# Selection of attended keys spread over the attention, and a feed-forward whose down projections lag one inner unit behind

## The chip, the cores and the metric

One core of a Trainium2 chip runs the whole program once. The metric is the time on the device in microseconds (us). PE is TensorE, DVE is VectorE, ACT is ScalarE, POOL is GpSimd, SP is SyncE.

## The reference

Two layers of a decoder trunk are applied to 1024 prompt tokens and 32 sample tokens (8 sequences of 4). Cut to what the change touches:

```
sc   = indexer_scores(q_idx, w_idx, k_idx)          # relu scores, weighted heads
sc   = where(key_pos <= pos, sc, -inf)
_, idx = top_k(sc, 256)                              # keys each token may attend
o    = softmax(q k[idx]^T / 8) v[idx]                # 8 query heads, 2 KV heads
...
x    = x + g1 * (concat[A, B, C] @ w_out)
h2   = rmsnorm(x) * (1 + sc2) + sh2
x    = x + g2 * (silu(h2 @ w_gate) * (h2 @ w_up)) @ w_down      # D = 1024, 2816 inner
```

`top_k` takes the earlier key where scores are equal. The kernel gathers no prompt keys: it adds a mask of 0 or -1e30 to dense logits.

## The kernel before, in words

All activations stand transposed: 8 tiles of 128 features by 1056 tokens, in three column chunks of 352 (TC). Each engine has its own instruction stream, and the order is written out by hand with semaphores. One loop runs over the two layers. `ended(engine, l, k)` (line 614) is a fence between stages: ACT and DVE each mark it, and whoever waits goes on only when both have. PSUM banks 0 to 2 form ring A, which ACT reads, and banks 3 to 5 ring Dr, which DVE reads; PE's `open` waits for a free bank, in order.

**Search.** For each token the 256th largest score is found bit by bit in 34 passes, on DVE (L1878) and ACT (L1403), for six blocks of prompt tokens (widths 384 to 1024; the first two blocks attend everything) and one array of sample scores (width 1056). It gives a threshold `thr` and `need`, how many keys equal to the threshold are still admitted.

**Selection.** Then DVE walks SEL_ORDER (L1945 to L1961), the sample first and after it the blocks from narrow to wide. For each it marks the scores equal to the threshold (L1952, for the sample L1949, with a count that PE sums over segments), numbers them with a scan (L1953), keeps those within `need` (L1957) and adds those above the threshold (L1960). ACT turns each result into a mask, (selected - 1) * 1e30, written over the scores (L1415). All three engines then pass fence 7 before the attention begins.

**Attention.** 32 turns p, block b = 7 - p//4, so from the widest block to the narrowest, four turns a block, one for each pair of heads. PE: `qk(p+1)` (L1071), `turns(p)` (transposes of the probabilities, L667), `pv(p-1)` (L1097), and from turn MASK_AT = 23 on `mask` (L1119), which expands the sample's mask. DVE: `logits(p+1)` (L1976: bank plus mask to SBUF, with the maximum), `turned(p)` (L1987), now and then `scales` and `heads`. ACT: `turned(p)` (L1432), `probs(p+1)` (exponentials, L1423). POOL meanwhile issues gathers of cached value rows, in order; the first four wait for the last use of the sample's key logits buffers.

**Products.** `product` (L703) multiplies 8 or nf tiles of 128 x 128 weights by 352 columns, three matmuls each (hi*hi, hi*lo, lo*hi of split fp32), chunk by chunk. The raw weights come by SP into one of two places; ACT writes their hi part (L1235) and DVE their lo part (L1512), and `unit_used`, counted by PE, says that the place's hi and lo parts are free again. `pair_by_tile` (L738) runs the first two products after a norm side by side, tile by tile, as the tiles of h arrive: once for w_in and once for the first gate and up products, in each layer.

**Feed-forward.** 22 inner units (gate product into ring A, up product into ring Dr), in blocks (0, 8), (8, 8), (16, 6) of FF_BLOCKS. For a unit ACT takes Silu of each gate chunk (L1473), DVE multiplies by the up chunk (L2089), ACT writes g_hi (L1478) and DVE g_lo (L2094), each into one of 8 tile slots. After a block PE waits for `g_ready`, which DVE marks behind the last g_lo, and then runs 8 down products over the block's tiles into ring Dr, which DVE adds to x (L2057).

Of the kernel before, what the change touches and what calls it, by code (L numbers as in the profile page):

```python
# [9 lines left out]
ALU = mybir.AluOpType  # L10
# [4 lines left out]
P = 128  # L15
# [14 lines left out]
BIG = 1e30  # L30
# [18 lines left out]
SEL_ORDER = (6, 0, 1, 2, 3, 4, 5)  # L49
# [119 lines left out]
FF_BLOCKS = ((0, 8), (8, 8), (16, 6))  # L169
TILES = 3 * KD + 3 * KF  # L170
UNITS = 18 + KD + sum(2 * n + KD for _, n in FF_BLOCKS)
# [122 lines left out]
def build(nc, a, o):  # L294
    ctx = ExitStack()
    with ctx:
# [87 lines left out]
        O_ROWIN, O_RMS, O_ACC, O_SQ = R(14), R(15), R(24), (R(22), R(21))  # L384
# [10 lines left out]
        MASK_USED = (1, 3, 4, 6)  # L395
        MASK_AT = 32 - 9
# [30 lines left out]
        def _(sp):  # L427
# [28 lines left out]
            with loop(sp, DEPTH, [units]) as l:  # L456
# [22 lines left out]
                for f0, nf in FF_BLOCKS:  # L479
                    with loop(sp, nf, [units]) as i:  # L480
                        unit(0, (to(0, KD, P), layer(wg, l)[:, :, bass.ds(i * P + f0 * P, P)]))
                        unit(1, (to(1, KD, P), layer(wu, l)[:, :, bass.ds(i * P + f0 * P, P)]))
# [6 lines left out]
        def _(pool):  # L489
# [30 lines left out]
            with loop(pool, DEPTH, [outs]) as l:  # L520
# [136 lines left out]
        def _(pe):  # L657
# [35 lines left out]
            def product(n, ring, hi, lo, n_k=KD):  # L693
# [3 lines left out]
                for c in range(3):  # L697
                    bank = ring.open()
                    for k in range(n_k):
                        w = slice(n % 2 * UNIT + k * P, n % 2 * UNIT + k * P + P)  # L700
                        x = slice(k * TOK + c * TC, k * TOK + c * TC + TC)
# [24 lines left out]
            def pair_by_tile(hi, lo, tiles):  # L726
# [4 lines left out]
                for k in range(KD):  # L731
                    pe.wait_ge(tile_lo, tiles + k + 1)
                    for u, ring in enumerate((A, Dr)):
                        w = slice(u * UNIT + k * P, u * UNIT + k * P + P)
                        for c in range(3):
                            x = slice(k * TOK + c * TC, k * TOK + c * TC + TC)
                            for m, (wt, xt) in enumerate(((w_hi, hi), (w_hi, lo), (w_lo, hi))):
                                mm = pe.matmul(banks[u][c][:, 0:TC], wt[:, w], xt[:, x], start=(k + m == 0), stop=(k == KD - 1 and m == 2))  # L738
                                if k == KD - 1 and u == 1 and c + m == 0:
                                    mm.then_inc(unit_used, 1)  # L740
                            if k == KD - 1:
                                ring.close(mm)
# [51 lines left out]
            with loop(pe, DEPTH, counts) as l:  # L794
# [268 lines left out]
                ended(pe, l, 7)  # L1063
# [58 lines left out]
                for p in range(32):  # L1122
# [7 lines left out]
                    if p >= MASK_AT:  # L1130
                        mask(p - MASK_AT)
# [60 lines left out]
                for f, (f0, nf) in enumerate(FF_BLOCKS):  # L1192
# [953 lines left out]
```

## Time and profile before

| | |
|---|---|
| three timed runs | 3782.92 to 3783.92 us, median 3783.87 |
| the profiled execution | 3765.66 us, its span 3763.8 |
| granted TensorE clock, mean | 0.91 of full speed |
| chain that ended last | PE 73%, DVE 9%, issue 7%, ACT 4%, DMA 4% |
| on that chain, L703 (products) | 53% |
| first layer: search, selection, attention | 590 to 752, 752 to 786, 786 to 947 us |
| first layer: feed-forward from the pair on | 1109 to 1885 us |

Read it so: the shares say that PE's products are most of the chain, but PE is busy 85% of the span, and the rest is spread over stages. What a change in a stage is worth is read from that stage's own stretch. The profiled execution ran 18 us under the median of the timed ones.

### The profile page before, as it was taken

How to read it: one execution, taken by the hardware profiler on the slowest of the kernel's cores; microseconds unless marked ns; L12 is line 12 of the kernel's file. 1: busy time of each engine (PE TensorE's matmuls, PEld its weight loads, DVE VectorE, ACT ScalarE, POOL GpSimd, SP SyncE). 2: the span in 40 equal slices, each digit the busy share in tenths (PEclk: the TensorE clock that was granted, in tenths of full speed). 3: DMA queues.
4: the chain of work that ended last, by engine and by line, in shares of the span. 5: the costliest groups of instructions: out<-in, count | busy, mean ns of one | idle time of the engine just before them, and what ended most of it. 6: DMA issues, size and time to landing. Idle time of an engine off the chain costs nothing.

```text
span 3763.8 us, 58485 instructions
## 1 busy us (share of the span) xinstructions
PE 3199.0 (85%) x20553; PEld 2738.8 (73%) x20553; DVE 1604.3 (43%) x3497; ACT 1182.9 (31%) x2081; POOL 258.6 (7%) x319
## 2 busy tenths in 40 slices
PE   3997677759889999999989867774889899999995
PEld 3994443235789999999979634332659899999995
DVE  3325568965342222222343355797534322222233
ACT  3122237835323212112231222584542321121121
POOL 1001022100200000000000101310020000000000
PEclk8997679979899999999999866897979899999997
DMA  5115025400411111111122321451041111111111
GB/s 178 39 39 198 12 77 171 145 7 18 169 34 45 45 45 50 40 50 43 42 48 43 112 109 47 140 163 45 18 158 45 34 45 45 45 48 47 45 38 53
DMA packets 275990, 261.19 MB, mean 69 GB/s; under 512 B 85513, under 2 KB 237567, under 8 KB 274513
## 3 DMA queue, kind: packets, MB, share of 16 engines
q1 hardware_dynamic: 244496, 155.76, 13.8%
q0 software_dynamic: 31312, 103.20, 8.4%
q8 instruction: 90, 1.47, 0.2%
q14 instruction: 92, 0.75, 0.1%
HBM read 249.33 MB, written 9.78 MB: 69 GB/s over the span
## 4 chain that ended last, share of the span: by engine, by line
PE 73%; DVE 9%; issue 7%; ACT 4%; DMA 4%; POOL 1%; DVEq 0%; ACTq 0%; SPq 0%; POOLq 0%
PE bank L703 53%; PE bank L667 4%; PE bank L738 2%; PE bank L1071 2%; ACT arena L1403 2%; PE bank L1097 2%; DMA weights<-in_w_ada 2%; DVE arena L1878 2%; PE bank L883 1%; DMA arena<-in_x_sample 1%; PE bank L1119 1%; PE bank L749 1%; PE bank L811 1%; PE bank L719 1%; PE bank L949 1%
## 5 line engine op out<-in xcount | busy, mean ns | idle before, releaser
L703 PE MATMUL bank<-h_hi,w_hi 128*128 128x352 f32 x2784 | 904.5, 325 | 9.8 <-DVE w_lo L1512 9.8
L703 PE MATMUL bank<-h_lo,w_hi 128*128 128x352 f32 x2784 | 894.4, 321 | 0.0
L703 PE MATMUL bank<-h_hi,w_lo 128*128 128x352 f32 x2784 | 894.2, 321 | 0.0
L703 PEld LDWEIGHTS bank<-h_hi,w_hi 128*128 128x128 f32 x2784 | 523.8, 188 | 12.6 <-issue 7.9
L703 PEld LDWEIGHTS bank<-h_lo,w_hi 128*128 128x128 f32 x2784 | 524.8, 188 | 1.7
L703 PEld LDWEIGHTS bank<-h_hi,w_lo 128*128 128x128 f32 x2784 | 523.3, 188 | 0.0
L1512 DVE TENSOR_TENSOR w_lo<-weights,w_hi 128x1024 fp32r<-128x1024 f32 x188 | 230.2, 1225 | 625.5 <-ACT w_hi L1235 620.0
L703 PE MATMUL bank<-g_hi,w_hi 128*128 128x352 f32 x1392 | 452.3, 325 | 16.6 <-DVE arena L610 16.6
L703 PE MATMUL bank<-g_lo,w_hi 128*128 128x352 f32 x1392 | 448.9, 322 | 0.0
L703 PE MATMUL bank<-g_hi,w_lo 128*128 128x352 f32 x1392 | 448.4, 322 | 0.0
L1235 ACT ACTIVATE w_hi<-weights 128x1024 fp32r<-128x1024 f32 x188 | 198.8, 1057 | 635.4 <-PE bank L703 583.0
L667 PEld LDWEIGHTS bank<-arena 128*128 128x128 f32 (+4 forms) x1773 | 216.3, 154 | 227.5 <-issue 174.5
L667 PE MATMUL bank<-arena 128*128 128x128 f32 (+4 forms) x1773 | 281.0, 299 | 112.7 <-DMA arena<-in_x_sample 23.8
L2057 DVE SCALAR_TENSOR_TENSOR stream<-bank,arena,stream 128x352 f32<-128x352 f32 (+1 forms) x192 | 109.6, 572 | 424.9 <-PE bank L703 417.1
L703 PEld LDWEIGHTS bank<-g_hi,w_hi 128*128 128x128 f32 x1392 | 263.1, 189 | 18.3 <-issue 18.3
L703 PEld LDWEIGHTS bank<-g_lo,w_hi 128*128 128x128 f32 x1392 | 263.7, 189 | 0.0
L703 PEld LDWEIGHTS bank<-g_hi,w_lo 128*128 128x128 f32 x1392 | 263.1, 189 | 0.0
L1878 DVE TENSOR_SCALAR_CACHE_REDUCE arena<-arena,srch 128x1056 bf16<-128x1056 int16 (+7 forms) x272 | 226.4, 884 | 11.8 <-DVE srch L1907 10.4
L1403 ACT ACTIVATE arena<-arena,srch 128x1024 bf16<-128x1024 int16 (+5 forms) x204 | 209.7, 1032 | 30.0 <-DVEq L1924 12.5
L2089 DVE TENSOR_TENSOR arena<-arena,bank 128x352 f32<-128x352 f32 x132 | 68.9, 522 | 314.1 <-PE bank L703 312.9
L1478 ACT ACTIVATE g_hi<-arena 128x352 f32 x132 | 65.8, 498 | 402.3 <-DVEq L2090 402.3
L1071 PE MATMUL bank<-arena 64*128 64x512 f32 (+3 forms) x384 | 95.7, 577 | 95.5 <-ACT arena L612 63.5
(327 smaller groups left out, 3711.4 us busy)
## 6 DMA issues: line engine op xcount, KB each, us to landing
weights<-in_w_ada SPq DMA_DIRECT2D x64, 512.0 KB, 7.0
weights<-in_w_gate SPq DMA_DIRECT2D x44, 512.0 KB, 3.7
weights<-in_w_up SPq DMA_DIRECT2D x44, 512.0 KB, 3.7
weights<-in_w_in SPq DMA_DIRECT2D x72, 256.0 KB, 3.5
arena<-in_w_ada SPq DMA_DIRECT2D x32, 512.0 KB, 4.3
weights<-in_w_down SPq DMA_DIRECT2D x32, 512.0 KB, 3.7
arena<-in_w_ada SPq DMA_DIRECT2D x8, 1024.0 KB, 18.2
weights<-in_w_down SPq DMA_DIRECT2D x16, 384.0 KB, 3.4
```

Source lines behind the costliest of these rows:

```text
L667: return pe.transpose(out, in_, C("ident", n, 0, 0, n))
L703: mm = pe.matmul(bank[:, 0:TC], wt[:, w], xt[:, x], start=(k + m == 0), stop=(k == n_k - 1 and m == 2))
L738: mm = pe.matmul(banks[u][c][:, 0:TC], wt[:, w], xt[:, x], start=(k + m == 0), stop=(k == KD - 1 and m == 2))
L1071: Dr.close(pe.matmul(banks[g][:, 0:w], S(R(R_Q + i, b * P), P, 64 * g, 64), S(R(R_K, c0), w, 64 * g, 64), start=True, stop=True))
L1097: mm = pe.matmul(B((XB, YB)[done % 2], [[1, P]], P * i, 64 * g, 64), S(O_VT + P * k + 64 * g, 64), S(O_PTT[p % 2][g] + P * k, P), start=(k ...
L1235: act.activation(w_hi[:, w], S(O_W + n % 2 * UNIT, UNIT), ACT.Copy).then_inc(unit_hi, 1)
L1403: act.activation(junk, digits(j, i), ACT.Sign, bias=srch[:, 0, j:j + 1], scale=-1.0, accum_out=S(M_CNT + j, 1)).then_inc(sign_counted, 1)
L1478: act.activation(g_hi[:, bass.ds(i * TOK + c * TC, TC)], S(R(17, c * TC), TC), ACT.Copy).then_inc(tile_hi, 1)
L1512: dve.tensor_tensor(w_lo[:, w], S(O_W + n % 2 * UNIT, UNIT), w_hi[:, w].bitcast(F32), ALU.subtract).then_inc(unit_lo, 1)
L1878: ins = dve.tensor_scalar(junk, digits(j, i), cand[:, j:j + 1], None, ALU.is_lt, ALU.add, accum_out=S(M_RAW if j == 6 else M_CNT + j, 1))
L2057: ins = dve.scalar_tensor_tensor(out=x, in0=bank[:, 0:w], scalar=S(O_MOD + 9 * (gate + j), 1), in1=x, op0=ALU.mult, op1=ALU.add)
L2089: read(dve.tensor_tensor(S(R(17, c * TC), TC), S(R(16, c * TC), TC), bank[:, 0:TC], ALU.mult))
```

## The change

The selection of the widest block alone stands before the attention; the others run in steps between DVE's attention turns (SEL_STEP), and ACT negates each in turn 2, 6, 10, 14, 18 or 22. PE no longer waits at fence 7. The scratch moves to four slots of the arena (R(5) to R(8)), where cached value rows were gathered early, so the first four value gathers now wait for the last mask. The feed-forward's blocks become (tiles of the down products) 7, 7, 8, with 8, 7, 7 inner units ahead of them, the tiles wrapping around the 8 slots. `pair_by_tile` runs the last two tiles of the first product before those of the second, and frees the first place when the second product's last two begin. The rows of the next layer's parameters land in R(23) instead of R(14).

```diff
-SEL_ORDER = (6, 0, 1, 2, 3, 4, 5)
+SEL_ORDER = (5, 4, 3, 2, 1, 0, 6)
+SEL_STEP = {0: ((1, 0), (1, 1)), 1: ((1, 2), (1, 3))}
+for _m in range(2, 7):
+    for _k in range(4):
+        SEL_STEP[4 * _m - 6 + _k] = ((_m, _k),)
-FF_BLOCKS = ((0, 8), (8, 8), (16, 6))
+FF_BLOCKS = ((0, 7, 8), (7, 7, 7), (14, 8, 7))
-        O_ROWIN, O_RMS, O_ACC, O_SQ = R(14), R(15), R(24), (R(22), R(21))
+        O_ROWIN, O_RMS, O_ACC, O_SQ = R(23), R(15), R(24), (R(22), R(21))
+        O_EQ, O_CUM, O_GT, O_EQS = (R(5 + n) for n in range(4))
...
                     if n < 4:
-                        pool.wait_ge(s_kv_used, l * 64 + 8 + K_TILES)
+                        pool.wait_ge(neg_ready, l * 7 + 7)
...
-                for k in range(KD):
-                    pe.wait_ge(tile_lo, tiles + k + 1)
-                    for u, ring in enumerate((A, Dr)):
...
-                                if k == KD - 1 and u == 1 and c + m == 0:
+                turns = [(k, u) for k in range(KD - 2) for u in range(2)] + [(k, u) for u in range(2) for k in range(KD - 2, KD)]
+                for k, u in turns:
+                    ring = (A, Dr)[u]
+                    if u == 0:
+                        pe.wait_ge(tile_lo, tiles + k + 1)
...
+                            if k == KD - 2 and u == 1 and c + m == 0:
+                                mm.then_inc(unit_used, 1)
...
                 count(PASSES, "earlier_seg", M_RAW + 1)
-                ended(pe, l, 7)
...
                     if p >= MASK_AT:
+                        if p == MASK_AT:
+                            pe.wait_ge(neg_ready, l * 7 + 7)
                         mask(p - MASK_AT)
...
-                for f, (f0, nf) in enumerate(FF_BLOCKS):
+                for f, (f0, nf, nu) in enumerate(FF_BLOCKS):
                     settle(pe)
-                    with loop(pe, nf - (f == 0), counts) as i:
+                    with loop(pe, nu - (f == 0), counts) as i:
                         product(0, A, h_hi, h_lo)
                         product(1, Dr, h_hi, h_lo)
                     pe.wait_ge(g_ready, l * 3 + f + 1)
                     settle(pe)
                     with loop(pe, KD // 2, counts) as i:
                         for n in range(2):
-                            product(n, Dr, g_hi, g_lo, nf)
+                            product(n, Dr, g_hi, g_lo, nf, f0 % KD)
...
-                for m, j in enumerate(SEL_ORDER):
+                def negated(m):
+                    j = SEL_ORDER[m]
                     act.wait_ge(sel_ready, l * 7 + m + 1)
-                    act.activation(neg_s if j == 6 else score(j), S(R(20 + m % 2), TOK if j == 6 else P * (j + 3)), ACT.Copy, bias=-BIG, scale=BIG).then_inc(neg_ready, 1)
+                    act.activation(neg_s if j == 6 else score(j), S(O_CUM, TOK if j == 6 else P * (j + 3)), ACT.Copy, bias=-BIG, scale=BIG).then_inc(neg_ready, 1)
+                negated(0)
                 ended(act, l, 7)
...
                 for p in range(32):
+                    if p % 4 == 2 and p < 24:
+                        negated(p // 4 + 1)
                     turned(p)
...
+                def select(m, k):
+                    j = SEL_ORDER[m]
+                    sc, n = score(j), P * (j + 3)
+                    eq, cum = S(O_EQ, n), S(O_CUM, n)
+                    if k == 0:
...
+                        step(dve.tensor_scalar(eq, sc, thr[:, j:j + 1], None, ALU.is_equal))
+                    elif k == 1:
+                        if m:
+                            dve.wait_ge(neg_ready, l * 7 + m)
+                        step(dve.tensor_tensor_scan(cum, eq, eq, 0.0, ALU.add, ALU.max))
+                    elif k == 2:
+                        step(dve.scalar_tensor_tensor(out=eq, in0=cum, scalar=need[:, j:j + 1], in1=eq, op0=ALU.is_le, op1=ALU.mult))
+                    else:
+                        dve.scalar_tensor_tensor(out=cum, in0=sc, scalar=thr[:, j:j + 1], in1=eq, op0=ALU.is_gt, op1=ALU.add).then_inc(sel_ready, 1)
+                def select_sample(k):
+                    eq, cum = S(O_EQS, TOK), S(O_CUM, TOK)
+                    if k == 0:
+                        dve.wait_ge(neg_ready, l * 7 + 6)
+                        step(dve.tensor_tensor_scan(cum, eq, eq, 0.0, ALU.add, ALU.max))
+                    elif k == 1:
+                        step(dve.scalar_tensor_tensor(out=eq, in0=cum, scalar=need[:, 6:7], in1=eq, op0=ALU.is_le, op1=ALU.mult))
+                    elif k == 2:
+                        dve.tensor_tensor(cum, eq, S(O_GT, TOK), ALU.add).then_inc(sel_ready, 1)
+                step(dve.tensor_scalar(S(O_EQS, TOK), score(6), thr[:, 6:7], None, ALU.is_equal, ALU.add, accum_out=S(M_RAW + 1, 1)))
+                dve.sem_inc(count_raw, 1)
+                for k in range(4):
+                    select(0, k)
+                step(dve.tensor_scalar(S(O_GT, TOK), score(6), thr[:, 6:7], None, ALU.is_gt))
+                dve.wait_ge(count_sum, (l + 1) * (PASSES + 1))
+                step(dve.tensor_tensor(need[:, 6:7], need[:, 6:7], XB[:, 0:1], ALU.subtract))
                 ended(dve, l, 7)
...
                 def logits(p):
                     b, i, done = PAIRS[p]
                     full = P * (b + 1)
+                    if i == 0 and b > 1:
+                        dve.wait_ge(neg_ready, l * 7 + NB - b)
...
                         heads(p // 4 - 1)
+                    for m, k in SEL_STEP.get(p, ()):
+                        if m < 6:
+                            select(m, k)
+                        else:
+                            select_sample(k)
...
+                def hidden(u, i, slot, signal=False):
...
+                    if signal:
+                        mark(dve, g_ready)
+                    split_lo(1)
+                for f, (f0, nf, nu) in enumerate(FF_BLOCKS):
+                    first = f0 + f
+                    if f == 2:
+                        hidden(f0 + 1, 0, KD - 1)
+                    whole = nf - 1 - min(f, 1) - (f == 2)
+                    with loop(dve, whole, counts) as i:
+                        hidden(first, i, i)
+                    hidden(first + whole, 0, whole, True)
+                    if f < 2:
+                        hidden(first + whole + 1, 0, whole + 1)
```

`hidden` on ACT and on DVE is the body of a unit as it was, with the tile's slot given by hand. SP's loops fetch the weights in the new order: 8, 7 and 7 gate and up pairs, and down products of 7, 7 and 8 tiles.

## Rows read from the trace of the kernel before

**Rows 1.** The page: busy time of the engines, share of the 3763.8 us span.

```profile
PE 3199.0 (85%) x20553; PEld 2738.8 (73%) x20553; DVE 1604.3 (43%) x3497; ACT 1182.9 (31%) x2081; POOL 258.6 (7%) x319
```

**Rows 2.** Stretches: us; busy PE, PEld, DVE, ACT, POOL; clock, DMA share, GB/s.

```profile
752.30:786.00 33.70, 0.58 (x2) 0.50 (x2) 31.29 (x33) 5.92 (x8) 0.00 (x0) 0.50 0.02 6
786.00:947.00 161.00, 139.46 (x1200) 88.26 (x1201) 84.49 (x320) 90.29 (x220) 4.50 (x5) 0.93 0.05 14
2574.00:2607.00 33.00, 0.58 (x2) 0.50 (x2) 30.90 (x31) 5.70 (x7) 0.00 (x0) 0.50 0.01 3
```

**Rows 3.** In order of time: start, us, engine, line, tiles, idle before and its releaser.

```profile
752.30 1.30 DVE L1949 TENSOR_SCALAR_CACHE_REDUCE arena<-arena,code 128x1056 f32<-128x1056 f32 x1
753.76 2.36 DVE L1953 TENSOR_TENSOR_SCAN arena<-arena 128x1056 f32<-128x1056 f32 x1
...
773.78 0.69 DVE L1952 TENSOR_SCALAR arena<-arena,code 128x896 f32<-128x896 f32 x1
...
776.56 1.15 DVE L1957 SCALAR_TENSOR_TENSOR arena<-arena,srch 128x896 f32<-128x896 f32 x1
...
778.93 0.75 DVE L1952 TENSOR_SCALAR arena<-arena,code 128x1024 f32<-128x1024 f32 x1
...
784.69 1.06 ACT L1415 ACTIVATE arena<-arena 128x1024 f32<-128x1024 f32 x1 [4.80 <-DVE arena L1960]
...
785.93 0.17 DVE L1964 MEMSET arena<- 128x128 f32 x1 [1.15 <-ACT arena L612]
...
788.34 0.69 DVE L1976 CUSTOM_DVE_ANT_0 arena<-bank,arena 128x512 f32<-128x512 f32 x1 [1.99 <-PE bank L1071]
```

**Rows 4.** Waits of DVE and ACT in the attention: total, times, longest.

```profile
DVE arena L1976 <- PE bank L1071: 51.0, 37, 2.4
ACT arena L1432 <- PE bank L667: 57.3, 34, 4.0
```

**Rows 5.** DVE in the attention, in brackets its idle time before the row.

```profile
802.17 0.69 DVE L1976 CUSTOM_DVE_ANT_0 arena<-bank,arena 128x512 f32<-128x512 f32 x1 [0.62 <-PE bank L1071]
...
809.09 0.69 DVE L1976 CUSTOM_DVE_ANT_0 arena<-bank,arena 128x512 f32<-128x512 f32 x1 [2.33 <-PE bank L1071]
...
899.72 0.69 DVE L1976 CUSTOM_DVE_ANT_0 arena<-bank,arena 128x512 f32<-128x512 f32 x1 [0.85 <-PE bank L1071]
...
902.61 0.56 DVE L1976 CUSTOM_DVE_ANT_0 arena<-bank,arena 128x384 f32<-128x384 f32 x1 [1.03 <-PE bank L1071]
...
905.91 0.56 DVE L1976 CUSTOM_DVE_ANT_0 arena<-bank,arena 128x384 f32<-128x384 f32 x1 [1.70 <-PE bank L1071]
...
908.58 0.56 DVE L1976 CUSTOM_DVE_ANT_0 arena<-bank,arena 128x384 f32<-128x384 f32 x1 [0.97 <-PE bank L1071]
```

**Rows 6.** ACT in the attention, before a pair's transposed tiles are copied.

```profile
912.39 0.87 ACT L1432 ACTIVATE arena<-bank 128x384 f32<-128x384 f32 x2 [0.40 <-PE bank L667]
```

**Rows 7.** Value gathers on the POOL queue.

```profile
748.39 0.93 POOL L573 DMA_INDIRECT arena<-in_cache_v,page_idx  x1 [0.30 <-issue]
```

**Rows 8.** Lines on TensorE: the down projections' products.

```profile
L703 PE MATMUL bank<-g_hi,w_hi 128*128 128x352 f32 x1392 | 452.3, 325 | 16.6 <-DVE arena L610 16.6
```

**Rows 9.** Ten us after three of the switches, and after the pair.

```profile
1302.70:1312.70 10.00, 9.92 (x52) 9.93 (x53) 2.25 (x3) 1.06 (x1) 0.00 (x0) 0.83 0.19 54
...
3126.20:3136.20 10.00, 9.96 (x45) 9.96 (x46) 1.81 (x2) 1.06 (x1) 0.00 (x0) 0.69 0.20 54
3406.70:3416.70 10.00, 9.94 (x61) 9.94 (x62) 2.40 (x3) 1.06 (x1) 0.00 (x0) 1.00 0.20 54
1136.80:1146.80 10.00, 9.93 (x46) 9.93 (x47) 3.95 (x7) 4.18 (x6) 0.00 (x0) 0.72 0.36 105
```

**Rows 10.** First layer, the end of the pair (L738) before the feed-forward's inner units.

```profile
1131.01 1.28 ACT L1473 ACT_TABLE_LOAD   x1 [8.03 <-PE bank L738]
...
1136.87 0.66 PE L703 MATMUL bank<-h_hi,w_hi 128*128 128x352 f32 x1 [3.68 <-DVE w_lo L1512]
```

**Rows 11.** The same at the pair before w_in's products.

```profile
109.70 0.42 PE L703 MATMUL bank<-h_hi,w_hi 128*128 128x352 f32 x1 [1.21 <-DVE w_lo L1512]
```

More of the change, by code:

```diff
@@ L168 @@
 K_TILES = NB * OCT
-FF_BLOCKS = ((0, 8), (8, 8), (16, 6))
+FF_BLOCKS = ((0, 7, 8), (7, 7, 7), (14, 8, 7))
 TILES = 3 * KD + 3 * KF
-UNITS = 18 + KD + sum(2 * n + KD for _, n in FF_BLOCKS)
+UNITS = 18 + KD + sum(2 * n + KD for _, _, n in FF_BLOCKS)
 INDEX_CHUNKS = [(b, c, min(512, P * (b + 1) - c)) for b in range(2, 8) for c in range(0, P * (b + 1), 512)]
@@ L478, in _ @@
                          (to(n, 4, P, 4 * P), w[512:1024].rearrange("(i p) n -> p i n", p=P)))
[L479 to L482, printed above, removed]
+                for f, (f0, nf, nu) in enumerate(FF_BLOCKS):
+                    u0 = f0 + (f > 0)
+                    with loop(sp, nu, [units]) as i:
+                        unit(0, (to(0, KD, P), layer(wg, l)[:, :, bass.ds(i * P + u0 * P, P)]))
+                        unit(1, (to(1, KD, P), layer(wu, l)[:, :, bass.ds(i * P + u0 * P, P)]))
                     with loop(sp, KD // 2, [units]) as i:
@@ L691, in _, with product @@
             counts.append(units)
-            def product(n, ring, hi, lo, n_k=KD):
+            def product(n, ring, hi, lo, n_k=KD, first=0):
                 pe.wait_ge(unit_lo, units.at(3))
@@ L2081, in _ @@
                 Dr.restart()
-                for f, (f0, nf) in enumerate(FF_BLOCKS):
-                    for turns in (nf - 1, 1):
-                        with (loop(dve, turns, counts) if turns > 1 else nullcontext(nf - 1)) as i:
-                            split_lo(0)
-                            for c in range(3):
-                                bank = Dr.next()
-                                dve.wait_ge(gate_ready, l * 3 * KF + i * 3 + (3 * f0 + c + 1))
-                                read(dve.tensor_tensor(S(R(17, c * TC), TC), S(R(16, c * TC), TC), bank[:, 0:TC], ALU.mult))
-                                dve.sem_inc(prod_ready, 1)
-                            for c in range(3):
-                                dve.wait_ge(tile_hi, l * TILES + i * 3 + (3 * KD + 3 * f0 + c + 1))
-                                t = bass.ds(i * TOK + c * TC, TC)
-                                step.only(dve.tensor_tensor(g_lo[:, t], S(R(17, c * TC), TC), g_hi[:, t].bitcast(F32), ALU.subtract))
-                            if turns == 1:
-                                mark(dve, g_ready)
-                            split_lo(1)
+                def hidden(u, i, slot, signal=False):
+                    split_lo(0)
+                    for c in range(3):
+                        bank = Dr.next()
+                        dve.wait_ge(gate_ready, l * 3 * KF + i * 3 + (3 * u + c + 1))
+                        read(dve.tensor_tensor(S(R(17, c * TC), TC), S(R(16, c * TC), TC), bank[:, 0:TC], ALU.mult))
+                        dve.sem_inc(prod_ready, 1)
+                    for c in range(3):
+                        dve.wait_ge(tile_hi, l * TILES + i * 3 + (3 * KD + 3 * u + c + 1))
+                        t = bass.ds(slot * TOK + c * TC, TC)
+                        step.only(dve.tensor_tensor(g_lo[:, t], S(R(17, c * TC), TC), g_hi[:, t].bitcast(F32), ALU.subtract))
+                    if signal:
+                        mark(dve, g_ready)
+                    split_lo(1)
```

65 lines of the change are left out of this document (28 added, 37 removed).

## The prediction

> **What bounds the kernel now.** I read the page first: PE is busy 3199 of 3763.8 us [rows 1], so about 565 us of the span are PE's idle time and only a stage's own stretch can tell which of it goes. The table by stretches comes next. Between the search and the attention there is a hole: 33.7 us with PE busy 0.58, while DVE is busy 31.3 [rows 2]; the second layer has the same hole. The order of instructions shows who holds it: DVE alone, from the sample's comparison at 752.30 to the widest block's last step, then ACT's negation at 784.69, the fence at 785.93, and the first logits leave their bank at 788.34, 36.0 us after the start [rows 3]. In the attention behind it PE is busy 139 of 161 us and DVE 84 [rows 2]; DVE stands 51.0 us waiting for PE's logits, in 37 waits of at most 2.4 [rows 4]. That idle time is the cover into which the selection is put. In the feed-forward PE runs without a hole except where it turns from inner units to down products: six waits on DVE's mark, 16.6 us in all, 2.77 each [rows 8], and after the pair, 3.68 us [rows 10].
>
> **The selection, what leaves the path.** Of the 31.3 us in the hole [rows 2] there remain in front: the sample's comparison with its readout, 1.46 (753.76 less 752.30), and the widest block, 5.76 (784.69 less 778.93) [rows 3]. New is the sample's "greater" comparison, costed as its "equal" one, 1.30, plus about 0.2 for the correction of `need`, 0.3 for marks and fence and 0.4 for preparing the small mask. Sum 9.4. ACT's negation of the widest block (1.06) lies beside the "greater" one. PE no longer stands at the fence, so its first logits, which took 2.3 us from 786.06 on, wait in the bank already. The first eviction comes 9.4 instead of 36.0 us after the start: 26.6 us saved in each layer.
>
> **What comes back in the attention.** The moved DVE work is 31.3 less 1.4, 5.7 and 0.2, so 24.0 us, in 23 instructions; with some 0.05 between dependent ones, 25 us. A step costs only what exceeds DVE's idle time before the next logits [rows 5]. Turn 0 gets the 896 wide block's first half, 2.78 (776.56 less 773.78) [rows 3], where 0.62 is idle: 2.2 lost. Turn 1 gets the second half, 2.37, against 2.33: 0.1. Turns 2 to 17 get one step each, the longest a scan of about 1.76 in turn 3, where the waits are like the 2.33 at 809.09; the tightest is turn 17, 0.62 in 0.85: nothing. Turns 18 to 20 get the sample's scan 2.36 and two more steps of about 1.3, with gaps 5.0, where 1.03, 1.70 and 0.97 are idle: 1.3. ACT's six negations take 0.5 to 1.06, where ACT waits 57.3 us in 34 waits before such copies, 1.7 each [rows 4]; but before turn 22's copies only 0.40 is idle [rows 6], so 0.7 for that one and nothing for the others. Together 4.3 us. The bounds: nothing, if PE had slack that I do not see, and 25, if no cover held. I take 4.3, as the idle times were read just where the steps land. Net 22.3 in each layer, 44.6 in both. What a late step holds up: DVE's next logits, behind them ACT's exponentials and PE's transposes. What is late next in front of the attention is DVE still, with its 9.4.
>
> The four value gathers on POOL (0.93 each, the last of them at 748 [rows 7]) now wait for the last mask, about turn 22, and the later ones queue behind them. Four times 1.24 is 5 us of POOL, with 33 us of attention left (912 to 947 [rows 2, 6]) and the DMA at a 0.05 share of its time [rows 2]. Costed at nothing; without that cover they would add 5 to the value stage.
>
> **The feed-forward.** The waits after the first and second block go, since PE has a whole unit (gate and up product, 23 us) to run while DVE finishes the tiles: 2 x 2 x 2.77 = 11.1 us. The third stays, as no unit is left to run ahead. With the waits goes what the clock takes after them: in the ten us after three of the four the granted clock is 0.83, 0.69 and, once, 1.00, with 52, 45 and 61 matmuls [rows 9] (the fourth, at 1582, is like the first). By the missing matmuls, 10 + 10 + 17 at 0.16 each, near 6.2 us more. So the clock was at its lower level, 1.2 GHz, for a time after an idle wait of 2.8, in three cases of these four. The work is otherwise the same: 22 units and 176 tiles of down product. The down products now follow an up product in the same ring, but DVE has read each bank two chunks (over 7 us) before it is wanted again, so nothing is added. More unrolled code on ACT and DVE: I put it at nothing, under the slack of a 11.5 us product.
>
> **The pair.** Ring A closes nine matmuls earlier and the first place is freed nine earlier: 9 x 0.16 = 1.43. In the feed-forward the wait of 3.68 hangs on ACT's table load and Silus, which start when the first gate chunk closes [rows 10], so it falls by 1.43. At w_in the wait of 1.21 [rows 11] hangs on the freed place and goes. Both layers: 2 x (1.43 + 1.21) = 5.3. The lower clock after the pair (0.72 [rows 9]) I leave; if the shorter wait spares it, 1.7 to 2.8 a layer more.
>
> **The sum.** 44.6 + 11.1 + 6.2 + 5.3 = 67.2 us, from the profiled 3765.66 to 3698.5. That execution lies 18.2 under the median of the timed runs; taken from the median, 3783.87 less 67.2 gives 3716.7.
>
> **Rivals.** **A, the selection is only half covered.** The idle times before the logits are not free room: a late eviction also holds back PE's transposes, and the delays add up over the turns. For it: the attention is a ring of three engines in which PE is busy 139 of 161 us, so PE catches up little. Against it: DVE's waits are on PE nearly all [rows 4]. With all 25 us exposed the saving falls by 2 x 20.7 to 25.8, 3758; half of it gives 3737.
> **B, the down projection finds another wait.** The change would not do what it says if the first down product waited for its split weights or for a bank of ring Dr that DVE reads late, since DVE now has a unit's work and the first residual close together. Then 11.1 + 6.2 = 17.3 stay: 3734. Against it: the same weights arrive in time between the products inside a block.
> **C, slower: the clock.** The attention's mean clock is 0.93, so about 22 of its 161 us run at 1.2 and the rest at 2.4 GHz [rows 2]. If the longer holes of turns 0 and 18 kept it at the lower, a wide turn (6.9 us, 802.17 to 809.09 [rows 5]) would take about 5 more, as its logits, transposes and products all double. To eat 33.6 us a layer this must hold for 7 wide turns; held through all the attention, PE's 139 us would grow by over 100 a layer, and the kernel would take about 3920. The trace speaks against it, as the clock stays up through the waits of every turn. The Trainium skill, "TensorE: Matmul & The Clock Gate", under "A second HAM failure mode: psum-queue depth-cycling", tells of a kernel that cycles through PSUM banks with short PE idles in between and so swings between the two clocks; by that rule this change, which adds such idles, risks C. The attention before has these idles already and mostly does not swing.
>
> **Chances.** The forecast 0.71, A 0.13 (in whole or half), B 0.08, C 0.04, the rest for mishaps that cost a few us. The range: down to 3702, if the selection costs nothing (8.6 less) and the clock after the pair is spared (about 5); up to 3738, which takes in B and half of A. A measurement of this kernel can tell about 0.2% from no change, 7.6 us; A and B lie beyond it too, on the faster side: faster 0.94, same 0.02 (A in whole with further losses), slower 0.04 (C).
>
> **What would show it.** Right: the hole before the attention under 12 us, DVE's first logits some 9 us after the sample's comparison, the attention 2 to 6 us longer than 159, two waits on the mark left in the whole feed-forward instead of six, the pair's waits 2.2 and near 0. Wrong: DVE waits in the attention that stay near 51 us while the stage grows by 20 (A); a new releaser in front of the first down product (B); a clock of 0.5 far into the attention (C).

## The result and the profile after

The changed kernel takes 3737.6 us (median of four runs, 3736.42 to 3742.96) where the kernel before takes 3783.39 on the same chip: ratio 0.9883, 95% interval 0.9866 to 0.9900, 45.8 us faster. The forecast was 67.2 us faster, 3716.7. The sign and the larger part of the mechanism hold, but 21 us of the forecast did not come: the range ended at 3738, a gain of 45.9 from 3783.87, and the measured gain lies just outside it. The two profiled executions, 3765.66 and 3736.81, differ by 28.8 only. Why that is less than 45.8 is an experiment's result too (e8).

The page of the changed kernel, busy time of the engines [rows 1 before]:

```profile
PE 3226.3 (86%) x20553; PEld 2749.4 (74%) x20553; DVE 1602.4 (43%) x3499; ACT 1182.4 (32%) x2081; POOL 257.9 (7%) x319
```

Its stretches (us; busy PE, PEld, DVE, ACT, POOL; clock, DMA share, GB/s): the hole, then the attention of the first and of the second layer [rows 2]:

```profile
760.12:769.39 9.27, 2.59 (x6) 1.00 (x6) 8.22 (x12) 1.15 (x2) 0.00 (x0) 0.50 0.00 0
769.39:938.30 168.91, 142.38 (x1189) 90.31 (x1189) 105.84 (x339) 94.14 (x225) 7.49 (x8) 0.89 0.08 26
...
2572.70:2743.40 170.70, 143.50 (x1190) 90.93 (x1190) 105.82 (x340) 94.42 (x225) 7.50 (x8) 0.89 0.08 26
```

The hole of 33.7 us is 9.3 now. DVE's work went from 84 to 106 us in the attention, and its waits for PE's logits in the first layer, 51.0 us before [rows 4], fell to 29.6, so most of the moved work did go into idle time (769.4 to 938.5; total, times, longest):

```profile
DVE arena L2020 <- PE bank L1079: 29.6, 31, 2.0
```

But the stage went from 157 (first logits 788.34 to first value transposes 945.5) to 169 and 171 us, not to the 161 of the forecast.

The head in order of time (start, us, engine, line, tiles, idle before and its releaser), to be read beside [rows 3]:

```profile
760.12 1.30 DVE L1997 TENSOR_SCALAR_CACHE_REDUCE arena<-arena,code 128x1056 f32<-128x1056 f32 x1
...
762.07 2.08 PE L1079 MATMUL bank<-arena 64*128 64x512 f32 x4
...
767.22 0.77 DVE L2001 TENSOR_SCALAR arena<-arena,code 128x1056 f32<-128x1056 f32 x1
767.34 1.06 ACT L1427 ACTIVATE arena<-arena 128x1024 f32<-128x1024 f32 x1 [10.82 <-DVE arena L1984]
...
769.39 0.69 DVE L2020 CUSTOM_DVE_ANT_0 arena<-bank,arena 128x512 f32<-128x512 f32 x1 [0.39 <-DVE arena L2007]
```

From the sample's comparison to the first logits' eviction 9.27 us, against 36.0 before and 9.4 forecast: the logits are computed from 762.07 on and wait in the bank; the "greater" comparison takes 0.77 and not 1.30.

Turn 0 and turn 22 are where the attention grew. DVE, ACT, PE and POOL at these two places:

```profile
782.18 2.02 DVE L1980 TENSOR_TENSOR_SCAN arena<-arena 128x896 f32<-128x896 f32 x1
784.43 0.69 DVE L2020 CUSTOM_DVE_ANT_0 arena<-bank,arena 128x512 f32<-128x512 f32 x1 [0.22 <-DVE arena L1980]
...
785.18 1.13 PE L1079 MATMUL bank<-arena 64*128 64x512 f32 x4 [3.30 <-DVE arena L2020]
786.24 3.53 PE L673 MATMUL bank<-arena 128*128 128x128 f32 x16
...
898.99 0.94 POOL L579 DMA_INDIRECT arena<-in_cache_v,page_idx  x1 [163.24 <-ACT arena L1427]
...
900.64 0.21 DVE L2024 TENSOR_REDUCE arena<-arena 128x1 f32<-128x1 f32 x2
...
906.22 0.69 DVE L2054 CUSTOM_DVE_ANT_0 weights<-bank,weights 128x512 f32<-128x512 f32 x1 [5.36 <-remote]
906.45 0.93 POOL L579 DMA_INDIRECT arena<-in_cache_v,page_idx  x1 [0.30 <-issue]
...
908.95 0.66 ACT L1446 ACTIVATE arena<-bank 128x256 f32<-128x256 f32 x2 [6.61 <-remote]
```

Turn 0: PE waits 3.30 us for the eviction behind the scan, and the 16 transposes after it take 3.53 us, at the lower clock (granted 0.54 from 788 to 790). Turn 22 has something that no row of before has: the last negation releases seven value gathers back to back (898.99 to 906.45), and DVE stands still for 5.36 us and ACT for 6.61, released by nothing that the profile shows. The chain of waits has it in both layers:

```profile
900.86 5.23 another core or an unknown queue
...
2706.39 5.18 another core or an unknown queue
```

While it lasts the DMA engines are full (stretches, columns as above; before, the share over the attention was 0.05 [rows 2]):

```profile
901.00:903.00 2.00, 2.00 (x17) 0.79 (x13) 0.00 (x0) 1.33 (x5) 1.39 (x3) 1.00 0.81 270
903.00:905.00 2.00, 1.65 (x20) 1.05 (x16) 0.00 (x0) 0.00 (x0) 1.60 (x2) 1.00 0.99 346
905.00:907.00 2.00, 0.03 (x1) 0.03 (x1) 0.78 (x3) 0.00 (x0) 1.49 (x2) 1.00 0.95 338
907.00:909.00 2.00, 1.20 (x3) 0.23 (x5) 0.89 (x7) 0.06 (x1) 0.38 (x1) 1.00 1.02 393
909.00:911.00 2.00, 1.56 (x14) 1.07 (x16) 1.61 (x8) 1.57 (x6) 0.00 (x0) 0.58 0.97 395
```

PE runs dry behind DVE (0.03 of 2 us) and its clock falls to 0.58. It comes back and falls once more before the stage ends:

```profile
909.00:913.00 4.00, 3.56 (x26) 2.52 (x28) 2.63 (x12) 1.89 (x7) 0.00 (x0) 0.57 0.57 230
913.00:919.00 6.00, 6.00 (x43) 2.86 (x43) 3.52 (x16) 3.78 (x14) 0.93 (x1) 1.00 0.29 87
919.00:938.50 19.50, 16.19 (x81) 8.14 (x80) 8.85 (x39) 10.39 (x35) 0.00 (x0) 0.51 0.00 1
```

The second fall is not the stall's: the kernel before has 0.51 in the last 19.5 us of its attention too, without a stall, where it was profiled once more on another chip (e8), and 0.88 in the profile on which the forecast rests.

The feed-forward and the pairs went by the forecast. By line, the down products [rows 8], and the first matmul after the pair [rows 10] and after w_in's pair [rows 11]:

```profile
L710 PE MATMUL bank<-g_hi,w_hi 128*128 128x352 f32 x1392 | 450.6, 324 | 5.5 <-DVE arena L616 5.5
```

```profile
1134.36 0.47 PE L710 MATMUL bank<-h_hi,w_hi 128*128 128x352 f32 x1 [2.25 <-DVE w_lo L1534]
...
107.84 0.37 PE L710 MATMUL bank<-h_hi,w_hi 128*128 128x352 f32 x1
```

The waits on the mark are 5.5 us in place of 16.6, the pair's 2.25 in place of 3.68, w_in's none in place of 1.21.

Two stages that the change leaves alone came out longer: the index-key stage (first to last gather of cached index keys) 64.6 us instead of 61.0, and the value stage (first value transpose, 938.5, to the first product of w_out, 995.3) 56.8 instead of 51.9.

### The profile page after: what moved, and what is told of

The parts are those of the page before. It is cut to its first block, busy times and chain, and to the rows that moved or that the text cites. A ratio compares the mean times of both kernels' runs of the same rounds, so it can differ in the third digit from the quotient of the medians.

```text
span 3735.0 us, 58431 instructions
## 1 busy us (share of the span) xinstructions
PE 3226.3 (86%) x20553; PEld 2749.4 (74%) x20553; DVE 1602.4 (43%) x3499; ACT 1182.4 (32%) x2081; POOL 257.9 (7%) x319
## 4 chain that ended last, share of the span: by engine, by line
PE 76%; DVE 8%; issue 7%; ACT 4%; DMA 3%; another core or an unknown queue 1%; DVEq 0%; POOL 0%; ACTq 0%; SPq 0%; POOLq 0%
PE bank L710 54%; PE bank L673 5%; PE bank L747 2%; PE bank L1079 2%; PE bank L1105 2%; ACT arena L1413 2%; DMA weights<-in_w_ada 2%; DVE arena L1900 2%; PE bank L1164 1%; PE bank L958 1%; PE bank L892 1%; DMA arena<-in_x_sample 1%; PE bank L758 1%; PE bank L1127 1%; PE bank L820 1%
## 5 line engine op out<-in xcount | busy, mean ns | idle before, releaser
L1413 ACT ACTIVATE arena<-arena,srch 128x1024 bf16<-128x1024 int16 (+5 forms) x204 | 209.8, 1032 | 29.9 <-DVEq L1946 12.4
L1494 ACT ACTIVATE g_hi<-arena 128x352 f32 (+1 forms) x132 | 65.8, 498 | 402.1 <-DVEq L2138 402.1
L1489 ACT ACTIVATE arena<-bank 128x352 f32<-128x352 f32 x132 | 61.4, 465 | 310.6 <-PE bank L710 309.5
```

The costliest lines, as they stand in the source:

```text
L1413: act.activation(junk, digits(j, i), ACT.Sign, bias=srch[:, 0, j:j + 1], scale=-1.0, accum_out=S(M_CNT + j, 1)).then_inc(sign_counted, 1)
L1494: act.activation(g_hi[:, bass.ds(slot * TOK + c * TC, TC)], S(R(17, c * TC), TC), ACT.Copy).then_inc(tile_hi, 1)
```

## The experiments

Each ratio is against runs of the kernel before on the same chip. The kernel before took 3768.3 us on the chip of e1 to e4, and 3797.6, 3797.2 and 3797.0 on the chips of e5 to e7, e8 to e11 and e12 to e14. No chip served for more than one of these groups, so "the chip" below stands for the chip together with all else that one group of runs shared. "Attention" is the stretch from DVE's first logits to PE's first value transposes, first and second layer.

### The parts one by one (e1 to e4)

**e1**: the kernel before, no edit.

> The kernel before, unchanged, profiled and timed once more. It tells whether the first profiled execution (3765.66 us, 18 us under the median of its timed runs) was a lucky one. Theory 1, the recorded execution escaped stalls that the others have: the new trace ends near 3783 and shows, beside the 3.7 and 2.8 us waits known, one or two idle times of about 5 us of DVE and ACT in each layer that end on something outside the cores' engines, as the trace of the changed kernel does at 568.71 (4.75) and 2375.28 (4.83) in code that the change leaves alone. Theory 2, profiled executions of this kernel run 18 us faster than timed ones throughout: the new trace ends near 3766 again and has no such stalls.

Measured: 3770.87 (3763.94 to 3774.14) against 3768.3, ratio 1.0003 (0.9993 to 1.0013). The profiled execution took 3772.2, index-key stage 61.2 us, attention 157.8 and 157.1, value stage 52.2, no idle time without a known releaser. Neither theory is settled by it: on this chip timed and profiled runs agree near 3768, and there are no stalls. The question went on to e8.

**e2**: the kernel before with all that the diff changes for the selection, its gathers' wait among it, and nothing in the feed-forward and the pair:

```
-SEL_ORDER = (6, 0, 1, 2, 3, 4, 5)
+SEL_ORDER = (5, 4, 3, 2, 1, 0, 6)
...
-                ended(pe, l, 7)
...
-                        pool.wait_ge(s_kv_used, l * 64 + 8 + K_TILES)
+                        pool.wait_ge(neg_ready, l * 7 + 7)
```

> The kernel before with the spread selection alone (feed-forward and pair as before). Theory 1, the parts add, the feed-forward and the pair give what was forecast (22) and the selection gave only what is left of 45.8: 24 us faster than before, ratio 0.9937, with a stall of about 5 us at turn 22 of each layer's attention and a value stage about 5 longer than before's 52. Theory 2, the selection gives its forecast 44.6 (0.988) and it is the other parts, or the three together, that lose 20.

Measured: 3723.82 against 3768.3, ratio 0.989 (0.9874 to 0.9907), 44.5 us faster, with an interval from 35 to 47.5: the forecast was 44.6, and the expectation of 24 was wrong. The attention takes 161.9 and 164.0 us. The same seven gathers stand back to back (888.17 to 895.63), but DVE's first mask of the sample waits 1.95 us, for PE:

```profile
891.99 0.69 DVE L2044 CUSTOM_DVE_ANT_0 weights<-bank,weights 128x512 f32<-128x512 f32 x1 [1.95 <-PE bank L1123]
```

The DMA engines are as full here as in the changed kernel, and PE and ACT go on:

```profile
896.00:898.00 2.00, 2.00 (x29) 1.49 (x25) 1.63 (x8) 0.74 (x3) 0.56 (x1) 1.00 1.02 395
```

So the selection's own sum was near, and the burst makes no stall on this chip. (This kernel differs from the changed one in more than the chip, and neither was run on the other's chip. e7 shows the burst in a third kernel, e12 and e13 compare with and without it on one chip.)

**e3**: the kernel before with the feed-forward's part of the diff alone (with `hidden`, `first` of `product` and SP's order of the weights).

```
-FF_BLOCKS = ((0, 8), (8, 8), (16, 6))
+FF_BLOCKS = ((0, 7, 8), (7, 7, 7), (14, 8, 7))
...
-                            product(n, Dr, g_hi, g_lo, nf)
+                            product(n, Dr, g_hi, g_lo, nf, f0 % KD)
```

> The kernel before with the feed-forward's blocks of 7, 7 and 8 and the next inner unit ahead of each down projection alone. Forecast of the step: 11.1 us of waits and 6.2 of clock, 17.3 in all, ratio 0.9954; the trace of the changed kernel gives 8.9 and 7.7 for the two layers' stretches, so 16.6. The rival, the new unrolled code on ACT, DVE and SP costs something outside the stretch (later fetches of instructions, weights landing late at the first unit): 5 us less than that, 0.9968.

Measured: 3753.44, ratio 0.9963 (0.9952 to 0.9974), 14.9 us faster. From the first product behind the pair to the last down product it takes 739.0 and 738.9 us, where e1 has 746.6 and 747.6: 16.3. The waits gone are the 11.1 forecast (5.5 left of 16.6). What is left for the clock is 3.8 us by the timed runs and 5.2 by the traces; the timed gain's interval, 9.8 to 18.1 us, does not exclude the 17.3 forecast.

**e4**: the kernel before with the order of the pair's last matmuls alone.

```
+                turns = [(k, u) for k in range(KD - 2) for u in range(2)] + [(k, u) for u in range(2) for k in range(KD - 2, KD)]
+                for k, u in turns:
```

> The kernel before with the other order of the last matmuls in the pair alone. Forecast: 5.3 us, ratio 0.9986; up to 2.8 a layer more if the shorter wait keeps the clock up, 11 us, 0.9971. The rival, something downstream of it (the next product waits for the same unit's weights) takes the gain: 0 us, 1.0000.

Measured: 3766.98, ratio 0.9996 (0.9987 to 1.0006). The waits did what was forecast:

```profile
1141.52 0.42 PE L703 MATMUL bank<-h_hi,w_hi 128*128 128x352 f32 x1 [2.25 <-DVE w_lo L1514]
```

but the time does not tell 5.3 us from nothing. Repeated as e14.

### The burst of gathers (e5 to e7)

**e5**: the whole change, no edit.

> The whole change once more, beside the kernel before. The kernel before ran at 3783 us where the change was first timed and at 3768 in the later runs. Theory 1, the change costs five-microsecond stalls of its own (turn 22 of each layer's attention, 5.2 us, seven value gathers back to back) wherever it runs: 44 to 46 us faster than before, ratio 0.988, and the stalls are in the trace. Theory 2, the stalls belong to the first place it ran and the parts add up: selection 0.989, inner unit 0.9963 and pair 0.9996 give 0.985, about 57 us faster, and the trace shows none.

Measured: 3744.18 against 3797.59, ratio 0.9868 (0.9851 to 0.9884), 53.4 us faster. The stalls of theory 1 are there again, DVE 12.4 us in two waits before the mask's eviction, ACT 13.5 in two; attention 170.7 and 171.3. The gain lies between those of the two theories.

**e6**: the order of the first eight value gathers.

```
-for n in range(K_TILES):
+for n in (4, 5, 6, 0, 1, 2, 3, 7) + tuple(range(8, K_TILES)):
```

> The whole change with the value gathers issued in another order: numbers 4, 5 and 6, whose places are free from turns 5, 13 and 17 on, ahead of 0 to 3, so that four and not seven follow each other at turn 22. Theory 1, the seven gathers back to back hold up what ACT and DVE fetch: the idle time of 5.2 us at turn 22 falls to 2 or less, 6 to 10 us faster than the whole change in both layers, unless the value stage takes it back. Theory 2, the burst has no cost: same time as the whole change within 3 us. The value stage (first transpose behind the fence to the first product of w_out) stays at 57 in both.

Measured: 3736.53, ratio 0.9847 (0.983 to 0.9863): 7.7 us under e5. Attention 165.5 and 165.2, and the wait before the first mask is shorter, not gone:

```profile
907.26 0.69 DVE L2054 CUSTOM_DVE_ANT_0 weights<-bank,weights 128x512 f32<-128x512 f32 x1 [4.03 <-remote]
```

**e7**: the kernel before, with the burst and nothing else of the change.

```
 if n < 4:
-    pool.wait_ge(s_kv_used, l * 64 + 8 + K_TILES)
+    pool.wait_ge(heads_read, l * 8 + 5)
```

> The kernel before with the first four value gathers held until turn 21 of the attention (a wait for the fifth head in place of the one for the last key tile), so that seven queue up there as in the change. Nothing else is moved. Theory 1, the burst costs a 5 us stall a layer in the attention: 10 us slower than before, 1.0027, with the idle time near turn 22. If besides it makes the value stage 5 longer: 20 us slower, 1.0053. Theory 2, hidden: 1.0000.

Measured: 3807.35, ratio 1.0033 (1.0018 to 1.0048), 9.8 us slower than before. Attention 164.6 and 163.9, with the stall at the same instruction (the first mask of the sample):

```profile
930.72 0.69 DVE L2010 CUSTOM_DVE_ANT_0 weights<-bank,weights 128x512 f32<-128x512 f32 x1 [6.67 <-remote]
```

So the burst alone makes the stall, in a kernel whose selection is untouched. The value stage takes 58.0 us here, which e8 explains otherwise.

### The chip, and versions without a burst (e8 to e11)

**e8**: the kernel before, no edit.

> The kernel before, unchanged, once more. Of the traces so far two kinds are seen. In one (before as first profiled, its repeat, the selection alone) the index-key stage takes 61 us from its first to its last gather and the value stage 52; in the other (the change twice, gathers apart, the gathers held in before) 65 to 67 and 57 to 58. Theory 1, this belongs to where the kernel runs and not to the change: with before near 3768 this trace shows 61 and 52, with before near 3783 to 3797 it shows 65 to 67 and 57 to 58, and its attention is 157 to 158 in either. Theory 2, only the changed kernels and the one with held gathers have it: 61 and 52 whatever the time.

Measured: 3797.03, ratio 0.9999. Index-key stage 66.4 and 66.9 us, value stage 57.4, attention 159.3 and 157.9: theory 1, with the first attention a little over it. Its stretches (attention, value stage), beside those of e1:

```profile
797.20:956.50 159.30, 139.24 (x1190) 88.08 (x1190) 83.77 (x317) 89.94 (x219) 3.76 (x4) 0.91 0.05 15
956.50:1013.90 57.40, 44.68 (x594) 28.68 (x594) 11.26 (x36) 18.10 (x33) 22.55 (x24) 0.80 0.75 242
```

```profile
791.70:949.50 157.80, 137.20 (x1190) 86.89 (x1190) 83.49 (x317) 89.97 (x219) 3.74 (x4) 0.93 0.05 15
949.50:1001.70 52.20, 38.98 (x594) 27.08 (x594) 11.35 (x36) 17.69 (x33) 22.50 (x24) 0.79 0.78 266
```

The longer index-key and value stages are there without the change, so they are no cost of it. And stalls without a known releaser are there without it too: in this trace ACT has two of 6 to 7 us in the second layer's index-key stage, among other gathers, where e1's has none.

```profile
2409.08 0.60 ACT L1392 ACTIVATE weights<-bank 128x512 f32<-128x512 f32 x1 [7.11 <-remote]
...
2418.55 0.60 ACT L1392 ACTIVATE arena<-bank 128x512 f32<-128x512 f32 x1 [6.43 <-remote]
```

Every trace from the three slower chips has such waits of DVE or ACT in that stage, the longest of each trace 5.0 to 7.1 us, and none of the four from the 3768 chip has one. The profile on which the forecast rests, with 61.0 and 51.9, looks like those of the 3768 chip. Against it the changed kernel's profile has 3.6 and 4.9 us more in the two stages, 17 us in two layers, which would account for the 18 us between that profile and its timed runs. That is argued and not shown, as no trace of the kernel before was taken in a 3783 run. The change's gain there is the timed 45.8, not 28.8.

**e9**: each of the first eight gathers at the turn where its place comes free.

```
-for n in range(K_TILES):
-    if n < 4:
+for n in (4, 5, 0, 6, 3, 1, 2, 7) + tuple(range(8, K_TILES)):
+    if n == 0:
+        pool.wait_ge(sel_ready, l * 7 + 6)
+    elif n == 3:
+        pool.wait_ge(sel_ready, l * 7 + 7)
+    elif n == 1:
         pool.wait_ge(neg_ready, l * 7 + 7)
+    elif n == 2:
+        pool.wait_ge(heads_read, l * 8 + 6)
     elif n < 8:
         pool.wait_ge(heads_read, l * 8 + MASK_USED[n - 4])
```

> The whole change with the first eight value gathers each at the turn where its place comes free: numbers 4 and 5 at turns 5 and 13, 0 and 6 at 17, 3 at 20, 1 at 22, 2 and 7 at 25. Theory 1, traffic that fills the DMA engines for some 10 us is what stalls ACT and DVE, and where no more than two gathers stand together there is no stall: the attention (first logits to the first value transposes) falls from 170 to 162 to 164 us, about 14 us in all against the whole change if it runs where the index-key stage takes 65 or more; 0 to 3 where it takes 61. Theory 2, only the number of gathers counts and not how they lie: no gain over the order 4, 5, 6, 0 to 3, 7 (165.3).

Measured: 3727.57 against 3797.19, ratio 0.9815 (0.9799 to 0.9832), 69.6 us faster. Attention 163.7 in both layers. Within the attention never more than two gathers stand together, and the first mask waits for PE, as in e2:

```profile
896.03 0.94 POOL L579 DMA_INDIRECT arena<-in_cache_v,page_idx  x1 [9.02 <-issue]
899.51 0.94 POOL L579 DMA_INDIRECT arena<-in_cache_v,page_idx  x1 [2.54 <-ACT arena L1433]
910.54 0.94 POOL L579 DMA_INDIRECT arena<-in_cache_v,page_idx  x1 [10.10 <-DVE arena L2050]
...
903.32 0.69 DVE L2060 CUSTOM_DVE_ANT_0 weights<-bank,weights 128x512 f32<-128x512 f32 x1 [1.95 <-PE bank L1133]
```

**e10**: e9, and less in turn 0.

```
-SEL_STEP = {0: ((1, 0), (1, 1)), 1: ((1, 2), (1, 3))}
-for _m in range(2, 7):
+SEL_STEP = {0: ((1, 0),), 1: ((1, 1),), 2: ((1, 2), (1, 3)), 3: ((2, 0),), 4: ((2, 1),), 5: ((2, 2), (2, 3))}
+for _m in range(3, 7):
...
-if p % 4 == 2 and p < 24:
+if p == 3 or p % 4 == 2 and 2 < p < 24:
     negated(p // 4 + 1)
```

> The paced gathers, and the 896 wide block's four steps laid on turns 0, 1, 2 and 2 in place of 0, 0, 1 and 1 (the next block's on 3, 4, 5 and 5; the negation of the first on ACT one turn later). Theory 1, turn 0 pays 2.2 us for its two steps, and the clock that falls behind the wait there pays 1 to 2 more: the attention falls by 2 to 4 us a layer against the paced kernel, 4 to 8 in all. Theory 2, the logits of turn 4 now wait for the later negation (1.0) and turn 2 is full (2.37 against some 2.3): the gain is 0 to 1 us a layer, not to be told from none.

Measured: 3729.75, ratio 0.9826 (0.9809 to 0.9842), 2.2 us over e9 with overlapping intervals: the time can't tell them apart. In the one profile, which is of the fastest of the four runs (3718.55), the attention does shrink, to 160.2 and 161.0 us, and after turn 0 the clock is up sooner. Ten us of e9, from 9.2 us after its first logits on, and the like of e10:

```profile
777.10:787.10 10.00, 6.70 (x26) 4.13 (x25) 6.28 (x14) 4.05 (x7) 0.00 (x0) 0.67 0.00 0
```

```profile
772.80:782.80 10.00, 8.77 (x70) 6.76 (x70) 6.95 (x20) 6.86 (x13) 0.00 (x0) 0.85 0.01 2
```

So turn 0 has some 3 us a layer in that profile, but no gain is shown in the timed runs.

**e11**: all value gathers behind the attention's fence.

```
 if n < 4:
-    pool.wait_ge(neg_ready, l * 7 + 7)
-elif n < 8:
-    pool.wait_ge(heads_read, l * 8 + MASK_USED[n - 4])
+    passed(pool, l, 8)
 elif n < 16:
     passed(pool, l, 8)
```

> The whole change with all value gathers behind the attention's last fence, so that none runs in the attention. Theory 1: the attention falls to 162 to 164 us as in the paced kernel, but the value stage waits for its first values: gathers are issued 1.24 us apart and land some 6 to 7 us after, so it grows by 6 us (landing of the first) to 12 a layer; in all 0 to 10 us slower than the whole change where that stalls, 12 to 24 where not. Theory 2, the stall in the attention has another cause than the gathers (the first use of the masks' code): it stays at turn 22.

Measured: 3749.73, ratio 0.9877 (0.9861 to 0.9894). Attention 161.7 and 161.8 without a stall, so its cause at turn 22 is the gathers and not the first use of the mask's code; the value stage pays with 69.3 and 67.4 us for 57:

```profile
769.60:931.20 161.60, 137.64 (x1189) 87.16 (x1189) 105.50 (x340) 94.22 (x225) 0.00 (x0) 0.93 0.01 1
931.20:1000.50 69.30, 48.87 (x594) 31.52 (x594) 11.27 (x36) 18.18 (x33) 29.95 (x32) 0.70 0.75 261
```

### Side by side on one chip (e12 to e14)

**e12**: the whole change. **e13**: e9's kernel. **e14**: e4's kernel.

> The whole change a third time. Two theories of what its gain hangs on. Theory 1: the attention pays a stall of 5 to 7 us a layer only where gathers stall the engines, which the index-key stage shows (65 to 67 us against 61); with before near 3768 and an index-key stage of 61 the gain is what the parts gave there, 0.989 + 0.9963 + 0.9996, 57 to 60 us, ratio 0.9845, and the attention 162 to 164; with before near 3797 it is 50 again, 0.987, and the attention 170. Theory 2: the parts do not add up anywhere: 0.987 at both.

Measured: 3745.89 against 3796.96, ratio 0.9865 (0.985 to 0.9879), 51.1 us faster; index-key stage 66.4, attention 168.5 and 171.2. Both theories expect 0.987 on such a chip, so this run does not tell them apart.

> The paced gathers once more, on the same chip as the whole change. Theory 1: where the index-key stage takes 65 to 67, 14 us faster than the whole change (0.9815 against 0.987); where it takes 61, within 3 us of it. Theory 2, the 14 us between the earlier runs were the place and not the kernel: within 3 us at either.

Measured: 3730.66, ratio 0.9824 (0.9809 to 0.9839), 66.3 us faster; attention 164.0 and 164.2. Against e12 on the same chip that is 15.2 us, so the pacing and not the chip makes the difference. The two attentions have 11.5 of it; where the rest lies is not shown.

> The pair alone, with more rounds. Its waits fell as forecast (1.21 to 0 and 3.68 to 2.25, 5.3 us in all) while the time fell by 1.3 with an interval from 4.9 less to 2.3 more. If the waits are worth what they measure: 0.9986. If the work behind takes it up again (weights of the next product, clock): 0.9996 again or above.

Measured: 3790.11, ratio 0.998 (0.9971 to 0.9989), 6.9 us faster. With e4's 1.3 it lies around the 5.3 of its waits, on both sides; the waits are gained, and more can't be said.

## Why the prediction was right and where it was wrong

- **The head of the attention**: right. 9.27 us for 9.4 forecast, 26.7 saved in each layer for 26.6. Inside the sum the "greater" comparison was put 0.5 too high, so part of the agreement is luck.
- **The moved steps, 4.3 us a layer**: the mechanism was right and the size a little low. On the 3768 chip the selection alone gained 44.5 us for 44.6 forecast, but that the two meet to 0.1 is luck: its attention grew from 157.8 and 157.1 (e1) to 161.9 and 164.0, 4.1 and 6.9, and with the 26.7 of each head that makes 42.4 by the traces. Two things in the sum were too small. By the prediction's own rule turns 18 to 20 cost 1.33, 0 and 0.3, so 1.7 and not 1.3. And the 2.2 of turn 0 was the wait alone; the transposes after it at the lower clock (3.53 us for 16, where 16 at 794.78, at full clock, took 1.97) were not in the sum.
- **"Four times 1.24 is 5 us of POOL ... Costed at nothing"**: this is the step that failed. I counted the queue's own time and the mean DMA share of 0.05, and missed two things. The moved wait also holds the three later gathers whose own waits are long over, so seven and not four fall together. And they fill the DMA engines (share 0.8 to 1.0 for some 10 us) in the middle of a stage in which three engines feed each other. On three chips this stalls DVE and ACT: e7 shows 9.8 us for the burst alone, e12 against e13 15.2 us within the change. In the first comparison the attention grew by 12.0 and 12.7 us for 4.3 forecast, 16 us too much, and that is most of the 21 that are missing. The range reached to 3738 through B and half of A, neither of which occurred; nothing in it stood for this.
- **The feed-forward**: 11.1 us of waits came out exactly. For the clock 3.8 to 5.2 us were measured and 6.2 forecast (e3: 14.9 in all for 17.3, a difference that the timed runs cannot tell from none). The prediction's own terms, 37 matmuls at 0.16, give 5.9 and not 6.2.
- **The pair**: its waits fell by 1.43 and 1.21 to the hundredth; the two timed gains lie on both sides of 5.3, 1.3 us (4.9 at most) and 6.9 (4.2 to 11.0).
- **The rivals**: A is out as a mechanism of the moved steps: the sign given for it was waits of DVE that stay near 51 us, and they fell to 29.6; with the steps and no stall the attention is 4 to 7 us longer and not 20 (e2). B is out, since the first down product waits for the mark once a layer as said, 5.5 us in all. C is out as it was told: the clock of the whole attention is 0.89 in the change and 0.92 in e9, and it is 1.00 from 797 to 817, right behind turn 0's spell. The stall has a short spell of its own (0.57 from 909 to 913), for which no term stood. The rule of the Trainium skill, "TensorE: Matmul & The Clock Gate", under "A second HAM failure mode: psum-queue depth-cycling", shows only as these spells, behind turn 0 and behind the stall, and at the stage's end, where the kernel before has it too (e8); a clock that swings through the stage does not show.
- **The reference time**: I took the median, 3783.87, less a sum read from an execution 18 us shorter. That was right if, as e8 suggests, the 18 us lie in stages the change does not touch. The sum of the parts on the 3768 chip is 44.5 + 14.9 + 1.3, 61 us; the whole change was not run there, so that it would gain 61 on that chip is not shown.

What stays open: what DVE and ACT wait for in the stall. The trace has a packet of an instruction queue in the same microseconds (8 KB at 903.85, and 16 KB at 898.52, just before the first gather), which fits engines that wait for code behind gathers; but on the 3768 chip such packets stand at the same places (8 KB at 893.36, 16 KB at 887.72 in e2) and no engine stalls. No experiment took the code fetches away. The Trainium skill, "DMA: Bandwidth & Descriptors", under "Queues, rings and completion order", says that a DMA engine goes round its queues and drains a packet of one before it turns to the next; by that rule a fetch could wait behind a gather's packet, and no run here shows it. Open too is the rest of the first comparison, 45.8 against 51 to 53 in e5 and e12, on a chip where the kernel before takes 3783, and why the chip of e1 to e4 shows neither the stalls nor the longer stages. The gathers themselves are no lighter there: the DMA share in the burst reaches 1.02 in both.

The kernel to keep is e9's: 0.9815 and 0.9824 of the kernel before in two comparisons, against 0.9868 and 0.9865 for the change.

## What to carry to other kernels

When a wait at the head of an in-order queue moves, list everything that queues behind it, with the time at which each would have gone by itself: what was spread over a stage may leave as one burst. Cost a burst by what it does to the engines' other traffic at its own place and not by the mean share of the stage, and give each transfer its own earliest release. Steps put into idle time one by one, read from the idle time in front of the very instruction that they delay, can be forecast to a few us.

## What the runs showed of the hardware that was not expected

- Seven gathers back to back, 128 x 1024 f32 each, (DMA share up to 1.0, 270 to 395 GB/s) left DVE idle for 5.4 to 6.9 us and ACT for up to 6.8 us, engines that do not use the gathered data, in every run that had them (the first comparison, e5, e7, e12) but the one on the 3768 chip (e2). ACT waits of 7.11 and 6.43 us of the same kind stand in the index-key stage of the unchanged kernel (e8).
- The same kernel took 3768.3 us on one chip and 3797.0 to 3797.6 on three others, in one group of runs each. Two gather-heavy stages account for most of it (21 of 29 us): 61 against 66 us and 52 against 57, in each of two layers.
- After PE's wait of 3.30 us in turn 0 the clock was at its lower level (1.2 GHz) again, 16 transposes in 3.53 us; after the waits of 2.77 in the feed-forward it was so in most cases and not in all [rows 9].
